# Expert layers of a 16-expert transformer: one expert at a time in split float32, or two at a time in plain float32

## What is computed

```python
g_sel = jnp.argmax(group_score, axis=-1)                 # best group of a token
top_w, top_i = lax.top_k(in_grp, TOP_K)                  # its two best experts, TOP_K = 2
for e in range(N_EXPERTS):                               # D = 1024, D_EXPERT = 512
    h = jax.nn.silu(xt @ w_gate[e]) * (xt @ w_up[e])
    y = y + gate[:, e:e + 1] * (h @ w_down[e])
```

## Time and profile before

| what | us |
|---|---|
| median of 3 executions (2123.26 to 2125.39) | 2125.27 |
| span of the profiled execution | 2120.6 |
| PE busy | 1994.9 |
| DVE busy | 1610.3 |
| ACT busy | 1126.7 |

### The profile page before, as it was taken

One profiled execution on the slowest core, in us unless ns is written; L12 is line 12 of the kernel. 1 busy time (PEld: TensorE's weight loads), 2 busy tenths in 40 slices (PEclk: granted clock), 3 DMA queues, 4 the chain that ended last, 5 costly groups with the idle time before them and its releaser, 6 DMA issues.

```text
span 2120.6 us, 24733 instructions
## 1 busy us (share of the span) xinstructions
PE 1994.9 (94%) x9388; PEld 1588.8 (75%) x9388; DVE 1610.3 (76%) x2023; ACT 1126.7 (53%) x1144; POOL 87.4 (4%) x136
## 2 busy tenths in 40 slices
PE   8999899999899997999998988899999788999997
PEld 5677688888647776888887875788888664788885
DVE  1787689889646868988886275889889654888987
ACT  1323366777322234767763363477777341676774
POOL 1111000000110110000000000000000000000000
PEclk9999899999999998999998999799999998899998
DMA  9777669999884854989994501588889521799994
GB/s 383 288 290 295 209 244 349 342 360 357 316 332 159 313 203 159 375 321 357 360 366 146 208 31 40 189 327 336 339 322 350 199 80 50 265 349 341 359 358 172
DMA packets 56414, 574.65 MB, mean 271 GB/s; under 512 B 5856, under 2 KB 9952, under 8 KB 24032
## 3 DMA queue, kind: packets, MB, share of 16 engines
q1 hardware_dynamic: 34704, 500.19, 62.3%
q0 software_dynamic: 15264, 59.78, 7.7%
q10 hardware_dynamic: 6320, 12.97, 1.8%
HBM read 569.77 MB, written 3.15 MB: 270 GB/s over the span
## 4 chain that ended last, share of the span: by engine, by line
PE 84%; DVE 11%; issue 3%; ACT 2%; DMA 0%; POOL 0%; POOLq 0%; ACTq 0%; DVEq 0%
PE bank L788 81%; DVE ring_parts L1950 3%; PE bank L820 2%; DVE work L1950 1%; DVE mix L2092 1%; DVE mix L1950 1%; ACT work L1464 1%; DVE small L1950 1%; ACT mix L1464 0%; DVE work_parts L1950 0%; ACT work_parts L1464 0%; PE bank L916 0%; DMA xT<-in_xT_in 0%; DVE oT L2128 0%; DVE small L2101 0%
## 5 line engine op out<-in xcount | busy, mean ns | idle before, releaser
L1950 DVE TENSOR_TENSOR ring_parts<-ring,hi_ring_parts 128x2048 fp32r<-128x2048 f32 x422 | 947.6, 2285 | 103.6 <-ACT hi_ring_parts L1464 102.9
L1464 ACT ACTIVATE hi_ring_parts<-ring 128x2048 fp32r<-128x2048 f32 x422 | 798.3, 1914 | 265.9 <-PE bank L788 190.3
L788 PE MATMUL bank<-hi_ring_parts,tokens 128*128 128x512 f32 x2048 | 662.9, 393 | 3.0 <-DVE mix L1950 1.7
L788 PEld LDWEIGHTS bank<-hi_ring_parts,tokens 128*128 128x128 f32 x2048 | 384.6, 188 | 85.0 <-DVE mix L1950 3.4
L788 PE MATMUL bank<-ring_parts,tokens 128*128 128x512 f32 x1024 | 399.1, 390 | 0.0
L788 PE MATMUL bank<-hi_ring_parts,work_parts 128*128 128x512 f32 x1024 | 326.4, 390 | 0.0
L1464 ACT ACTIVATE work<-bank 128x512 f32<-128x512 f32 (+6 forms) x207 | 108.6, 527 | 285.0 <-PE bank L788 273.4
L788 PEld LDWEIGHTS bank<-hi_ring_parts,work_parts 128*128 128x128 f32 x1024 | 192.3, 188 | 40.1
L788 PEld LDWEIGHTS bank<-ring_parts,tokens 128*128 128x128 f32 x1024 | 192.6, 188 | 37.6
L788 PE MATMUL bank<-ring_parts,work_parts 128*128 128x512 f32 x512 | 199.3, 389 | 0.0
L788 PE MATMUL bank<-ring,xT 128*128 128x512 f32 (+2 forms) x352 | 139.2, 555 | 1.8 <-DVE xT L2481 1.8
(11 more groups left out here) (232 smaller groups left out, 2257.4 us busy)
## 6 DMA issues: line engine op xcount, KB each, us to landing
ring<-in_weights SPq DMA_DIRECT2D x237, 2048.0 KB, 8.7
hi_ring<-in_ada POOLq DMA_DIRECT2D x38, 512.0 KB, 12.0
mod_rows<-in_ada POOLq DMA_DIRECT2D x25, 512.0 KB, 5.9
work<-in_ada POOLq DMA_DIRECT2D x22, 512.0 KB, 6.0
work<-in_vecs POOLq DMA_DIRECT2D x8, 1024.0 KB, 5.5
mix<-in_ada POOLq DMA_DIRECT2D x11, 512.0 KB, 5.5
work<-bias_rows ACTq DMA_DIRECT2D x4, 1024.0 KB, 8.0
ring<-in_weights SPq DMA_DIRECT2D x2, 1024.0 KB, 8.0
```

Of the source, the lines that this page charges most:

```text
L788: ins = nc.tensor.matmul(o, lhsT, rhs, start=start, stop=stop)
L1464: return nc.scalar.activation(o, i, f, **kw)
L1950: return v.tensor_tensor(o, a, b, op)
```

## The change

Two experts are computed at a time. Each has room for 64 tokens: the first's are columns 0 to 63 of the stationary operand and write output partitions 0 to 63, the second's are columns 64 to 127 and partitions 64 to 127. Matmuls of the two alternate chunk by chunk. A pair is a "round". All expert products are plain float32 (`nc.tensor.matmul` on float32 operands), one in place of three; ACT and DVE no longer split expert weights, tokens or hidden values. Gather and scatter still use split values.

A piece of a pair now holds half of the chunks of both experts, and comes in two loads of 1 MB. Since `hi_ring` is free in an expert stage, its room makes two more slots: six in an expert stage, four elsewhere. Pieces in memory are in plain order of experts.

Layers 0 and 1 have 8 rounds. Layers e and o have 9: experts 0 and 1 as a pair, then the two of the others with the most tokens alone, each with 128 columns, then six pairs in falling order of counts. DVE sorts the counts (`positions`), and SP reads the order before it loads the third expert (`order_ready`). Every round has its own scatter, and gathers are made for two rounds at a time (five sets a layer). Tokens for which there is no room are computed behind the stage by a branch over all 16 experts and all 256 tokens.

```diff
 RING = 4
+SLOTS = 6
+CAP = P // 2
+def rounds_of(tag):
+    pair = [(p, p + 1) for p in range(0, NEXP, 2)]
+    return [pair[0], (2,), (3,), *pair[2:]] if tag in SORTED else pair
+def round_order(n):
+    order = [("g", 0), ("u", 0), ("d", 0), ("g", 1), ("u", 1)]
+    for r in range(1, n - 1):
+        order += [("g", r + 1)] + ([("d", r), ("u", r + 1)] if r < n - 2 else [("u", r + 1), ("d", r)])
+    return order + [("d", n - 1)]
...
+def ring_slot(j):
+    return ring[:, j, :] if j < RING else \
+        hi_plain[:, 2 * (j - RING):2 * (j - RING) + 2, :].rearrange("p a b -> p (a b)")
...
-                        for c in range(DC // 2):
-                            t = (slice(None), DC // 2 * h + c, slice(None))
-                            ins = three(o, tok_hi[b][t], tok_lo[b][t], hi[:, c, :], lo[:, c, :],
-                                        h == 0 and c == 0, h == 1 and c == DC // 2 - 1)
+                        of = sides(what, r, h, DC)
+                        for k, c in enumerate(of[0][0]):
+                            for _, cols, w in of:
+                                ins = mm(o[cols, :], tokens_of(tag, r)[:, c, cols], w[:, k, :], c == 0, c == DC - 1)
+                        release[0] += 2
...
+                            for _, cols, w in of:
+                                ins = mm(o[n][cols, :], ehT[:, r % 2, c, cols], w[:, k, n * 512:(n + 1) * 512],
+                                         c == 0, c == HC - 1)
...
+                gather(0)
+                places(0)
+                gate(0)
+                gate_up("u", 0)
+                gather(1)
+                places(1)
+                turn_hidden(0)
+                down(0)
+                gate(1)
+                gate_up("u", 1)
+                scatter(0)
+                for r in range(1, last):
+                    two = len(kinds[r + 1]) == 2
+                    gate(r + 1, (0,)) if two else None
+                    turn_hidden(r)
+                    gate(r + 1, (1,) if two else None)
+                    if r < last - 1:
+                        down(r)
+                        if gathered_ahead(tag, r):
+                            gather(gathered_ahead(tag, r))
+                            places(gathered_ahead(tag, r))
+                        gate_up("u", r + 1)
+                        scatter(r)
+                    else:
+                        gate_up("u", r + 1)
+                        down(r, (0,))
+                        turn_hidden(r + 1)
+                        down(r, (1,))
+                down(last, (0,))
+                scatter(last - 1)
+                down(last, (1,))
+                scatter(last)
...
-            def split_expert(tag, j, halves=(0, 1)):
-                for half in halves:
-                    part = Half(tag, j, half)
-                    dve.wait_ge(hi_ready, part.n)
-                    tt(part.lo, part.raw, part.hi, ALU.subtract).then_inc(lo_ready, 1)
...
+                picks(0)
+                gathered(0)
+                if tag[0] in SORTED:
+                    positions(tag)
+                banks.wait_full(dve, f"{tag}.sg0")
+                picks(1)
+                without_place(tag)
...
+            def load_expert(tag, m, found):
+                for p in ROUNDS[tag][r]:
+                    if tag in SORTED and p >= 2 and p not in found:
+                        sp.wait_ge(order_ready, k + 1)
+                        found[p] = sp.value_load(order[0:1, k * NEXP + p:k * NEXP + p + 1], min_val=0, max_val=3 * (NEXP - 1))
+                if NEED[m]:
+                    sp.wait_ge(halves_done, NEED[m])
+                for a, p in enumerate(ROUNDS[tag][r]):
+                    sp.dma_start(dest, src).then_inc(full, 16)
```

More of the change, by code:

```diff
@@ L93, in split_halves, with ring_plan, hi_free @@
                 halves += [2 * m, 2 * m + 1]
[L94 to L121, removed]
+    return halves, parts
+SPLIT_HALVES, PARTS = split_halves()
+def ring_plan():
+    slot, full, need = [], [], []
+    held, landed = [-1] * SLOTS, [0] * SLOTS
+    for tag in TAGS:
+        first, linear = MOE_FIRST[tag], LINEAR[tag]
+        last_split = max(PARTS[f"{tag}.{name[:-1]}"][0] for name in linear if name.endswith("/"))
+        for m in range(first - len(linear), first + NMOE):
+            if m == first:
+                held[RING:] = [last_split] * (SLOTS - RING)
+            usable = range(SLOTS) if m >= first else range(RING)
+            j = min(usable, key=lambda k: held[k])
+            pair = m >= first and len(ROUNDS[tag][MOE_PIECES[tag][m - first][1]]) == 2
+            landed[j] += 32 if pair else 16
+            slot.append(j)
+            full.append(landed[j])
+            need.append(2 * (held[j] + 1))
+            held[j] = m
+    return slot, full, need
+SLOT, FULL, NEED = ring_plan()
+def hi_free(n):
+    after_moe = max([2 * (MOE_FIRST[tag] + NMOE) for tag in TAGS if MOE_FIRST[tag] < SPLIT_HALVES[n] // 2], default=0)
+    before = SPLIT_HALVES[n - HI_RING] + 1 if n >= HI_RING else 0
+    return max(after_moe, before)
 UROW = 512
@@ new lines, in experts, with gather @@
+                    (NEXP, 2 * NEXP, P, [(every, r_in[:, 0, :]), (cs("before"), r_in[:, 1, :])]),
+                    (2 * NEXP, 3 * NEXP, P, [(every, r_in[:, T, :]) for T in range(NT)])])
+                def gather(j):
+                    pe.wait_ge(pick_ready, NT * (2 * (5 * layer + j) + 1))
+                    for name, c0, per, width in gather_jobs(tag, j):
+                        product(name, [(c * width, (c + 1) * width, P,
+                                        [(src[:, T, (c0 + c) * P:(c0 + c + 1) * P], pick_parts[:, T, 0:width])
+                                         for src in (src_hi, src_lo(tag)) for T in range(NT)]) for c in range(per)])
@@ L1688, in experts @@
-                y_hi(sets - 1)
+                gathered(0)
+                places(0)
+                sig(0)
+                gathered(1)
+                places(1)
+                hidden(0)
+                y_hi(0)
+                sig(1)
+                for r in range(1, last):
+                    hidden(r)
+                    sig(r + 1)
+                    if r == last - 1:
+                        hidden(r + 1)
+                    y_hi(r)
+                    if gathered_ahead(tag, r):
+                        gathered(gathered_ahead(tag, r))
+                        places(gathered_ahead(tag, r))
@@ L2914, in put_experts @@
     def put_experts(g, u, d):
[L2915 to L2917 removed]
+        for k in range(NEXP):
+            for w in (g, u, d):
+                put(chunks(w[k]))
     for l in range(DEPTH):
```

969 lines of the change are left out of this document (344 added, 625 removed).

## The result

The changed kernel takes 1918.39 us, the median of four executions (1916.06 to 1919.13); four executions of the kernel before, on the same chip, have a median of 2124.57 us. The ratio is 0.9032, with a 95% interval of 0.9019 to 0.9044. The forecast was 1889 us in a range of 1850 to 2045. 206 us went, of 236 forecast.

A forecast was written before the change was run, and what follows sets the result against it. PE bounds the kernel before; after the change DMA bounds layers 0 and 1, and both bound e and o. Stages save 245 us, smaller parts +6 - 15: 236 off 2125.3 gives 1889 us, own range 1850 to 1930, with rivals to 2045.

The forecast's parts named there:

- Halves in parallel, 0.858 us a product pair: Expert products: both column halves run at once, so a pair of products takes 0.858 us, a round 20.6 us.
- The sign that was named: PE's timeline, if right: alternating halves start 0.429 us apart for each half, 0.215 between any two.
- rival 1: Expert products: the halves follow each other, a round takes 41.2 us, PE bounds, about 2470 us in all; chance 0.17.
- rival 2: Expert products: halves overlap, but two of four weight loads are exposed, round 27.1 us, about 2040 in all; chance 0.12.
- the smaller parts: Mostly outside the expert stages: 6 us saved before the router, 15 lost to late first pieces at three borders.
- rival 3: Expert stages: DMA stays at 366 GB/s, stages of 252 and 255 us, 1992 in all; chance 0.12.
- DMA at 420 GB/s, 5.0 us a piece: Loads in expert stages: with several always queued, DMA runs at 420 GB/s, 5.0 us for each of 42 pieces.
- The start of a stage: Layers 0 and 1: PE frees its first slot after 4 x 0.858 = 3.4 us, then the 42 loads follow.
- The prediction's step: PE's clock in expert stages: waits are under 2 us a piece, so clock drops were priced at 0.
- the 85 us: Layers e and o: PE's need up to the third round's end, by when 20 pieces are loaded.
- The 3.5 us of friction: Stages e and o: added because PE and DMA both bound there, 231.5 and 229.5, giving 235 us.
- Nothing for DVE's sort: Layers e and o: the sort's 5.5 us on DVE and SP's wait of about 3 us are covered, costing nothing.

The follow-up runs named there:

- kept_busy: The changed kernel plus dummy plain float32 matmuls, results unread, in PE's idle time before each expert stage (five of 512 columns, two of 256): 1895.75 us, ratio 0.8934.
- pairs_only: The changed kernel with layers e and o as eight pairs, leaving out tokens beyond an expert's 64 and their branch: 1880.35 us.

## Why the prediction was right, point by point

**Halves in parallel, 0.858 us a product pair: right.** Starts of the halves are 6 ns apart and steps 0.429. The sign that was named, 0.215 between any two starts, did not come: the two halves start together and not in turn. The key step, that two plain float32 streams together read the moving operand at nearly the rate of one fp32r stream (2 x 512 columns in 0.429 us against 512 in 0.227, 6% faster), was an argument, and the runs show the overlap, not its reason; without halves the price is the one that rival 1 was given, 2463.83 against 2470. "TensorEngine Tiling (Array Packing)" of the Trainium skill (Key Properties) says that different tiles work in parallel, and the trace agrees for two column halves in plain float32. Of the drain that it names at a change of tiling mode little is seen: eight instructions of halves start at 467.77 us, the transposes on all columns behind them at 469.59, and 4 x 0.429 = 1.72 of the 1.82 between is their own.

**Weight loads hidden (against rival 2): right.** A load of 64 columns takes 133 to 149 ns, and steps stay at 0.429. The price of this rival, 2040, left out the +6 - 15 of the smaller parts, which rival 3 has; with them its own terms give about 2055.

**DMA at 420 GB/s, 5.0 us a piece (against rival 3): right.** The stages' slices show 421; by the packets of the trace the 42 pieces of the first stage take from 286.25 to 496.98 us, 5.02 each. The figure of about 358 GB/s in "DMA: Bandwidth & Descriptors" of the Trainium skill (Measured) is each core's rate when both cores of a memory stream. One core ran here, at a rate 18% above it, so this case does not test that figure, and the 2010 worked out from it was no rival for one core. The 366 of the earlier trace rows was no limit of DMA but nearly PE's own pace: an expert was three pieces, 6.29 MB, in 16.37 us of products and 0.6 of transposes, 371 GB/s. That takes the ground from rival 3, and from 5.73 us as a bound. Why the DMA share was 0.96 at that rate stays open.

**The start of a stage: the term that was mis-sized.** Layer 0 was 3.4 + 209.6 + 7.5 = 220.5; measured it is 8.0 (the stage's start to the first packet) + 210.7 + 8.7 = 227.4. The 3.4 was PE's work on one piece at full clock, 8 x 0.429, and it failed in three ways.

First, PE enters the stage at 1.2 GHz: in layer 0 the granted clock rises 5.1 us after the start, which costs half of that, 2.6 us. In layers 1, e and o it rises after 3.3, 2.5 and 5.4 us. The prediction's step said that the clock would hold because waits in the stage are short; it looked at the inside of the stage and not at its edge. In the kernel before the first gather was 32 matmuls of 256 columns, and the clock rose within it: its steps fall from 0.21 to 0.12 us. Two of its rows, between those of the earlier trace rows:

```profile
271.08 1.05 PE L788 MATMUL bank<-work_parts 128*128 128x256 f32 x4
271.94 1.02 PE L788 MATMUL bank<-work_parts,x_parts 128*128 128x256 f32 x4
```

Now it is 32 of 128 columns, its steps stay at 0.21 to the end, and the rank product ahead of it stands behind a wait of 7.06 us in place of 5.11:

```profile
266.84 2.32 PE L747 MATMUL bank<-work,consts 128*128 128x16 f32 x10 [7.06 <-DVE work L1779]
275.74 0.63 PE L747 MATMUL bank<-work_parts,x_parts 128*128 128x128 f32 x2
276.16 0.63 PE L747 MATMUL bank<-work_parts 128*128 128x128 f32 x2
```

Which of the two, the longer wait or the smaller gather, keeps the clock down is not shown; that work in the waits brings it up is (kept_busy).

Second, PE tells SP of a free slot with the next product (`mm` raises `halves_done`), about 1.1 us after the piece is done: with dummies, at full clock, SP issues the first load 4.5 us after the start, not 3.4. Third, from issue to the first packet there is 1.0 us (7.1 to 8.0 without dummies, 4.5 to 5.5 with them). 3.4 + 2.6 + 1.1 + 1.0 is the 8.0, but for rounding.

The tail is 1.2 longer. The last packet moves at 496.98 us, the last of its semaphore updates comes at 498.61, and PE begins the piece at 499.41, behind a scatter: 2.4 us where 1 was taken, a value that no row had. A stage of pairs is longer than forecast by 6.9 and 6.2 us in layers 0 and 1, and by 7.1 and 6.0 in the e and o of pairs_only: 26 of the 32 us that the stages missed by. Some 17 of these are the start, 5 the tails, 4 the pieces at 5.02 in place of 4.99.

**Layers e and o: right in kind, short by little.** They were to be 14.5 us longer than 0 and 1, and are 15.7 and 18.9 longer than the same stage in pairs. After the 85 us that the prediction gave PE up to the third round 20 pieces were to be loaded; by the packets it is 18.1 in e and 17.8 in o, as the loads stop with a full ring. Moving the experts alone back takes 6 and 8 us. The 3.5 us of friction stood on no row, and no run shows them apart.

**Smaller parts: +9 as forecast, by luck: two errors cancel.** The router was to be shorter by 6 us. The removed split did free DVE (its `x_parts` starts at 256.40 us in place of 258.30), but the rank product now waits for the choice of the top two, so it starts at 266.84 us in place of 264.26, and the halved gather takes 7.1 us in place of 5.7. On the other side, the linear parts were to lose 15 us to late first pieces; what lies between the stages grew by only 2.3, 4.6, 1.0 and 1.1 us, router included.

**Nothing for DVE's sort: right.** The order is written at 1249.1 us, 2.3 us after stage e begins; SP issues the first load of the stage at 1252.8, as the first slot comes free, so nothing waits for the order.

**The span.** The median lies 2.1 us above the span now; 4.7 was taken. The sum of the miss is then +31.9 in the stages, 0 outside, -2.6 around the span, 29.3 in all.

## What to carry to other kernels

When two results are too narrow to fill TensorE's columns, run them in column halves even if that takes a slower number format; the format without the halves would have lost here. When PE stops being the bound, recount what its busy work had done besides: here the clock had risen before each stage began. A stage bound by loads also pays for the whole way from the last use of a buffer to the first data of its next load: the release, the issue and the start of the transfer. And long work on the compute side should stand where the buffers are empty, not where they are still full.

## What the runs showed of the hardware beyond this

- PE begins a matmul of one column half ahead of up to three earlier ones of the other. Four instructions of the other half in between cost 0.05 us a piece; eight cost 1.77 in a piece that stands alone, with the second half four instructions late. "TensorE: Matmul & The Clock Gate" of the Trainium skill (Part 3) has matmuls in strict order; for two halves the starts at 333.054 and 333.060 speak against it.
- An fp32r matmul of 128 columns costs what one of 256 does: 0.11 us a step at 2.4 GHz against 0.12, and 0.21 both at 1.2 GHz. Halving the columns of the gather saved nothing.
- Seven matmul calls of no use, in a wait, took 5.6 us off a layer on average: 7.9 in layer 0, 6.4 in 1, 4.6 in e and 3.4 in o.
- A load's last packet and the matmul that waits for it lay 1.8 us apart (477.05 and 478.87 us).
